# S5 layer: three blocks of inputs transposed ahead of the first state products

## The reference, cut to what matters

```python
bu = jnp.einsum('blgc,gpc->blgp', u_blk.astype(jnp.complex64), b_bar)   # inputs drive the states
bu = bu.at[:, 0].add(lam_bar * h)
_, hs = lax.associative_scan(_linear_combine, (a, bu), axis=1)          # h[t] = lam_bar*h[t-1] + bu[t]
y = jnp.real(jnp.einsum('blgp,gcp->blgc', hs, c_c)) + d_g * u_blk
```

## Time and profile before

| | |
|---|---|
| median of 3 runs | 1072.84 us (1072.24 to 1074.46) |
| the profiled execution, its own time | 1072.88 us |
| its span, from first to last instruction | 1071.1 us |
| TensorE busy | 941.1 us, 88% |
| VectorE / GpSimd / ScalarE busy | 416.5 / 377.4 / 196.7 us |
| mean granted TensorE clock | 0.956 |
| stage of the S5 products | about 579 to 651 us of the span |

### The profile page before, as it was taken

How to read it: one execution, slowest core, us unless ns; L and a number is a source line. 1 busy time by engine, 2 the same in 40 slices (tenths; PEclk the granted TensorE clock), 3 DMA queues, 4 the chain that set the end, 5 groups by cost and what they waited for, 6 DMA issues and landing times.

```text
span 1071.1 us, 15922 instructions
## 1 busy us (share of the span) xinstructions
PE 941.1 (88%) x5748; PEld 576.7 (54%) x5748; DVE 416.5 (39%) x921; ACT 196.7 (18%) x386; POOL 377.4 (35%) x647
## 2 busy tenths in 40 slices
PE   4999989999988887888887599999989998778786
PEld 3888879554654443444444485445556554434442
DVE  4500355786542322223137771132564232121227
ACT  4413221222200000000035431003331000000003
POOL 1378910382266676665642730000021111101100
PEclk9999999999799999989998799999969999999998
DMA  7127841550689999999982946430076999999965
GB/s 258 44 76 281 338 166 42 220 196 31 275 330 415 427 422 423 411 400 409 401 335 87 154 135 269 202 145 32 25 292 257 423 420 425 427 422 424 424 251 201
DMA packets 45922, 292.30 MB, mean 273 GB/s; under 512 B 10737, under 2 KB 12017, under 8 KB 26391
## 3 DMA queue, kind: packets, MB, share of 16 engines
q1 hardware_dynamic: 35463, 270.18, 64.0%
q0 software_dynamic: 8640, 16.03, 4.0%
q10 hardware_dynamic: 1760, 5.31, 1.6%
HBM read 270.36 MB, written 36.80 MB: 287 GB/s over the span
## 4 chain that ended last, share of the span: by engine, by line
PE 55%; DMA 26%; DVE 5%; SPq 4%; POOL 4%; issue 4%; ACT 2%; POOLq 1%; DVEq 0%; ACTq 0%
DMA arena<-in_w_gu 17%; PE ps L752 13%; PE ps L1039 10%; PE ps L895 8%; PE ps L1266 5%; DMA arena<-in_w_down 4%; POOL arena L2429 3%; PE ps L1029 3%; SPq L576 2%; PE ps L966 2%; PE ps L925 2%; PE ps L1191 2%; PE ps L1198 2%; DMA arena<-scratch_kp 2%; PE ps L714 1%
## 5 line engine op out<-in xcount | busy, mean ns | idle before, releaser
L1039 PE MATMUL ps<-arena 128*64 128x256 f32 x2048 | 243.1, 394 | 47.1 <-DMA arena<-in_w_gu 46.9
L1039 PEld LDWEIGHTS ps<-arena 128*64 128x64 f32 x2048 | 150.6, 142 | 140.3 <-issue 40.9
L2330 POOL TENSOR_TENSOR arena<-arena 128x32 f32<-128x32 f32 (+5 forms) x232 | 118.1, 509 | 161.7 <-DMA arena<-in_s_d 67.0
L2429 POOL TENSOR_TENSOR arena<-arena 128x256 f32<-128x256 f32 (+3 forms) x192 | 131.8, 686 | 40.5 <-POOL arena L2429 40.0
L752 PE MATMUL ps<-arena 128*128 128x256 f32 (+1 forms) x640 | 142.1, 383 | 0.3 <-ACT arena L1378 0.3
L1029 PE MATMUL ps<-arena 128*64 128x512 f32 x512 | 122.2, 619 | 14.7 <-DMA arena<-in_w_down 14.2
L752 PEld LDWEIGHTS ps<-arena 128*128 128x128 f32 x640 | 121.0, 190 | 19.1 <-ACT arena L1378 0.5
L2073 DVE TENSOR_TENSOR arena<-arena,ps 128x128 f32<-128x128 f32 x64 | 18.4, 287 | 254.6 <-ACT arena L1521 251.1
L895 PE MATMUL ps<-arena 128*128 128x512 f32 x256 | 114.6, 597 | 1.0 <-DMA arena<-in_w_out 0.9
L1521 ACT ACTIVATE arena<-ps 128x128 f32<-128x128 f32 x64 | 17.7, 277 | 468.5 <-PE ps L1039 468.5
L1029 PEld LDWEIGHTS ps<-arena 128*64 128x64 f32 x512 | 36.7, 141 | 78.6 <-issue 65.0
(11 more groups left out here) (225 smaller groups left out, 993.6 us busy)
## 6 DMA issues: line engine op xcount, KB each, us to landing
arena<-in_w_gu SPq DMA_DIRECT2D x64, 2048.0 KB, 12.4
arena<-in_w_down SPq DMA_DIRECT2D x64, 1024.0 KB, 14.5
arena<-in_w_in SPq DMA_DIRECT2D x10, 1024.0 KB, 6.9
scratch_yd<-arena SPq DMA_DIRECT2D x2, 4160.0 KB, 17.9
arena<-scratch_yd SPq DMA_DIRECT2D x16, 512.0 KB, 7.4
arena<-in_w_out SPq DMA_DIRECT2D x1, 4096.0 KB, 12.3
scratch_hd<-arena ACTq DMA_DIRECT2D x8, 512.0 KB
arena<-in_w_glu SPq DMA_DIRECT2D x2, 2048.0 KB, 7.9
```

The source lines that it names most:

```text
L1039: mm = pe.matmul(ps[CAP * f:CAP * f + CAP, 2 + s, 0:256], XT[l][:, kc, CAP * s:CAP * s + CAP], WGU[l][i][s][:, kc, 256 * f:256 * f + 256], ...
L2330: step(g_.tensor_tensor(out, a, b, op))
L2429: g_.tensor_tensor(o, x, y, f).then_inc(sem("matrix_steps"), 1)
```

## The change

The third block of inputs is transposed before the first state products, and each later block one place earlier; the list of PSUM jobs follows. The new TensorE order is u0, u1, u2, zs0, u3, zs1, u4, zs2, u5, zs3, u6, u7, zs4 to zs7. Instructions, copies and transfers are the same in number and kind. The orders written for ScalarE, VectorE, GpSimd and SyncE stay as they are. SyncE's wait for ("zs", 3) stands for one more job of the list than before, since u5 is now ahead of it.

```diff
-    j += [(("k", 0), "act"), (("k", 1), "act"), (("us",), "dve"), (("u", 0), "act"), (("u", 1), "act"), (("zs", 0), "dve")]
+    j += [(("k", 0), "act"), (("k", 1), "act"), (("us",), "dve")] + [(("u", q), "act") for q in range(3)] + [(("zs", 0), "dve")]
     for q in range(1, 4):
-        j += [(("u", q + 1), "act"), (("zs", q), "dve")]
-    j += [(("u", q), "act") for q in (5, 6, 7)] + [(("zs", q), "dve") for q in (4, 5, 6)]
+        j += [(("u", q + 2), "act"), (("zs", q), "dve")]
+    j += [(("u", q), "act") for q in (6, 7)] + [(("zs", q), "dve") for q in (4, 5, 6)]
...
-            in_chunks(0)
-            in_chunks(1)
+            for q in range(3):
+                in_chunks(q)
             driven(0)
             for q in range(1, 4):
-                in_chunks(q + 1)
+                in_chunks(q + 2)
                 driven(q)
-            for q in (5, 6, 7):
+            for q in (6, 7):
                 in_chunks(q)
             for q in (4, 5, 6):
                 driven(q)
```

## The result

The changed kernel takes 1080.23 us (median of 15 runs, 1077.02 to 1092.60), the kernel before 1074.05 us in the same comparison. The ratio is 1.0067, 95% interval 1.0045 to 1.0089: slower by about 7 us, clear of noise. One of the 15 runs of the kernel before took 2400.38 us, for a reason that no trace shows; it doesn't move the median. I had forecast 1072.8 us, no change.

What follows compares the result with a forecast made beforehand. In the S5 stage TensorE waits until 613.2 for the taps of half 0, a transfer. Gains of -0.5 us at zs3 and -1.8 at zs7 are given back there: 0.0 us, forecast 1072.8 us, range 1071.0 to 1074.6.

Steps and rivals of the forecast that it cites:

- Steps (1) to (4): S5 stage, TensorE's order: u2 into idle time, u copies earlier, driven(3) 0.5 us, zs4 1.5, driven(7)'s end 1.8 us earlier.
- Step (5): TensorE's wait for the taps of half 0: they land at 613.2 in either kernel, so the gain is 0.0 us.
- They still do.: DMA queues: ScalarE's requests for half 1 still stand behind SyncE's earlier ones, so their earlier release costs nothing.
- The prediction's own sign of this: New profile: taps landing after 614, with q10 packets before 609, would show that ScalarE's queue cut in.
- The rival: ScalarE's queue cuts in, sharing evenly with half 0's remaining taps from the start: +8 us, 1080.8 us; chance 3%.
- its condition: Slower case decides once ScalarE's requests are served before SyncE's fourth tap, more than 2.3 us of shared service.
- The taps land when issued: SyncE's line has room, so the earlier issue after driven(3) comes through: -0.5 us, 1072.3 us; chance 5%.
- The clock: TensorE: full speed possibly before 591, 0 to -2 us, hidden in the wait; from_inputs starts as slowly as before.

Runs made afterwards that it cites:

- Experiment 5: Kernel before, with only tap 4 of half 0 issued ahead of the turn matrices instead of behind them: 1080.73 us, ratio 1.0051.
- 6: Changed kernel, with ScalarE issuing its taps of half 1 only once the turn matrices have landed: 1077.47 us, ratio 1.0012.
- 7: Changed kernel, with TensorE's last block of state products, driven(7), waiting for the first scan: 1077.25 us, ratio 1.0014.
- 9: Changed kernel, with SyncE issuing all taps of half 0 first and the turn matrices last: 1085.78 us, ratio 1.0103.
- after_guard: Changed kernel, with ScalarE issuing its taps of half 1 only once all taps of half 0 have landed: 1077.16 us, ratio 1.0017.
- before_guard: Kernel before, with ScalarE issuing its taps of half 1 only once all taps of half 0 have landed: 1075.44 us, ratio 1.0010.
- old_again: Kernel before, unchanged, executed once more for its queues: 1075.73 us.
- after_two_queues: Changed kernel; ScalarE issues taps 4 to 7 of half 0 early, SyncE the others; ScalarE's half 1 waits for half 0's landing: 1081.39 us, ratio 1.0054.
- experiment 8: The same run as after_two_queues, half 0 of the taps issued on two queues in the changed kernel: 1081.39 us, ratio 1.0054.

## Why the prediction was wrong

- **Steps (1) to (4) held.** u2's transposes lie in the idle stretch (2.33 us of it are left of 3.10), `driven(3)` starts 7.65 us after `driven(0)` instead of 7.94, and the end of `driven(7)` is 1.8 us earlier against the start of `driven(0)`. `driven(3)` gained 0.3 us rather than 0.5, because `driven(1)` ran wholly at the lower clock (mean granted clock 0.50 over it, 0.60 before), 2.19 us instead of 1.93.
- **Step (5) failed**, that the taps land at 613.2 in either kernel because the order of requests stays, and with it the sentence it leans on: "They still do." I took q10's 8 silent microseconds for a line in which ScalarE's requests stand behind SyncE's by order of issue, and concluded that 1.8 us could not matter, with SyncE's last tap issued more than 3 us ahead. The order of issue is in fact unchanged, and q10 cuts in all the same. What the runs showed in its place: the taps land 5.9 us later, and the order of issue does not by itself make a line across the two queues. Whether q10 starts after 4.6 to 5.5 us or only behind the taps of half 0 goes, in every profile here, with what q1 is moving when the requests come. Experiment 5 made the loss in the old kernel, 6 and 7 took it out of the new one, 9 made ScalarE's issue early with no cut. The prediction's own sign of this (landing after 614, q10 packets before 609) is what the trace shows.
- **The rival had the right mechanism and nearly the right size**: it gave 1080.8 us, measured are 1080.23. That the number fits so well is partly luck: its 8 us were four taps at half the rate, but 2.2 taps were left when q10 started; the last of the 16 counts of half 0 then came 1.8 us behind the others (0.9 before), and the engines were out of step, with packets of half 1 already moving on some: q1 moved 0.94 MB up to the landing, and only 0.58 MB of half 0 were left. What was wrong is its chance, 3%, and its condition. (The chances as written add up to 102%.) I had excluded it by a rule that the trace shows in one constellation only. The page of the Trainium skill that I set against the trace ("DMA: Bandwidth & Descriptors", "Queues, rings and completion order": the engines take turns among queues with work) describes the changed kernel from 607 on, 0.06 and 0.05 MB in a microsecond. Against it, `turns_last` shows 10 us in which a queue with requests issued got no turn.
- **"The taps land when issued"** played no part: the 0.3 us gained at `driven(3)` is not found at the landing in any run.
- **The clock**: the mean granted clock during TensorE's wait is 0.63 (this row, ahead of the DMA share and GB/s), much as before (0.61 in the earlier trace rows). `from_inputs` took 8.71 instead of 9.56 us, at a mean granted clock of 0.82 instead of 0.75, which took back 0.85 us.

```profile
601.20:620.06 18.86, 0.00 (x1) 0.01 (x1) 14.77 (x18) 0.00 (x0) 12.77 (x14) 0.63 1.05 170
```

Two things stay open. First, what in the issuing or the fetching of requests makes the difference; the traces show when packets start, not when a request reaches an engine. Second, a remainder: the variants of the changed kernel without the cut lie at 1.0012 to 1.0017 (1.0025 with one queue), each interval but the last reaching to 1 or below. In them the turn matrices land late. In `after_guard`, where q10 was silent, VectorE waits for them until 608.14:

```profile
608.14 1.42 DVE L1671 TENSOR_TENSOR arena<-ps,arena 128x512 f32<-128x512 f32 x2 [4.37 <-DMA arena<-scratch_turns]
```

The semaphore events show 15 of the 16 counts of this transfer in by 605.3 and one at 608.1. At the landing of half 0 the last count is 0.2 to 0.9 us behind the one ahead of it in the first profile of the kernel before, in `before_guard` and in `after_wait_turns`, and 1.0 to 2.3 us in all other executions, `before_t4_first` and `old_again` among them. In `after_guard` the 15 others are in 22.5 us after the first issue, about as before (22.2), in the changed kernel only after 27.2 (29.0 for the last). So of the 6 us by which the landing is later there, 5 are common to all counts and go with the sharing, 1 is the straggler. That the new order brings the straggler on is not shown.

No version beat the kernel before. The new order removes waits that another wait covers, so even with ScalarE held back nothing was won.

## What to carry to other kernels

Before a gain ahead of a covered wait is costed at nothing, list the transfers that it releases earlier and ask whether the transfer that ends the wait is still moving then: here 1.8 us of earlier release cost 6 us of shared DMA engines. A load that nobody needs soon is best released by the landing of the one that somebody does need, not only by the event that frees its buffer; this is one wait on an idle engine. And that a second queue is silent in one trace is a fact about that moment, not a rule of order, until the moment has been shifted.

## What the runs showed of the hardware

- SyncE's and ScalarE's queues share the DMA engines about evenly (0.94 and 0.93 MB in the changed kernel), but not from the issue on. With taps of half 0 still in SyncE's line, ScalarE's first packet came 4.6 to 5.5 us after its issue when 1 MB in 8 KB packets was moving or about to move in the first queue, and 6.9 to 10.1 us after it when at most the last 37 of its 128 packets had yet to begin, or none of it was moving. With half 0 landed (`after_guard`, `before_guard`) it came 3.4 and 5.8 us after, when at most some 30 packets of SyncE's line had yet to begin; and 1.5 us after where both queues began together (`after_two_queues`).
- Taps in 2 KB packets moved at 0.13 MB/us on one queue at a share above 1, the turn matrices in 8 KB packets at 377 GB/s (0.377 MB/us) in `after_two_queues` from 606 to 608, at a share of 0.97. By share and count a packet of 2 KB takes about 0.25 us in the earlier trace rows, and one of 8 KB has a median of 0.31 us: four times the bytes in 1.2 times the time. The taps are limited by their packets, not by their bytes.
- Two queues together moved taps at 198 GB/s in one place, at 169 in another (`after_two_queues`) and at 141 in the changed kernel's cut (606.84 to 620.06), against 125 to 130 for one; for experiment 8 I had counted on 200. What sets this rate is not shown.
